# Expert layers of a two-layer decoder: the first pair's token rows are fetched from DRAM like those of the other seven pairs, instead of being packed by matrix products, and all row numbers are formed ahead of the pairs

## What is computed

```
lc   = xf @ w_coarse + b_coarse          # 4 groups; the best one is taken, with its softmax weight
lf   = (xf @ w_fine + b_fine)[that group]  # 4 experts of the group; the best two, softmax over the two
comb = sum of one_hot(expert) * weight   # [280 tokens, 16 experts], two entries a row
h    = silu(xf @ w_gate[e]) * (xf @ w_up[e])     # 1024 -> 256, for each expert e
y    = sum over e of (h * comb[:, e]) @ w_down[e]  # 256 -> 1024
```

## Time and profile before

| | |
|---|---|
| median of three runs | 1041.59 us |
| the profiled execution | 1038.86 us |
| its span, first to last instruction | 1037.2 us |
| mean granted clock of TensorE | 0.904 of 2.4 GHz |
| PE busy | 905.3 us (87%) |
| DVE busy | 462.8 us (45%) |
| ACT busy | 238.0 us (23%) |
| POOL busy | 180.1 us (17%) |
| moved by DMA | 165.33 MB, mean 159 GB/s |
| experts of layer 0, first gate product to last down product | 266.3 to 394.3 us |
| experts of layer 1, the same | 874.7 to 1003.5 us |

### The profile page before, as it was taken

How to read it: one execution, slowest core, us unless ns; L and a number is a source line. 1 busy time by engine, 2 the same in 40 slices (tenths; PEclk the granted TensorE clock), 3 DMA queues, 4 the chain that set the end, 5 groups by cost and what they waited for, 6 DMA issues and landing times.

```text
span 1037.2 us, 17012 instructions
## 1 busy us (share of the span) xinstructions
PE 905.3 (87%) x6716; PEld 669.5 (65%) x6716; DVE 462.8 (45%) x1015; ACT 238.0 (23%) x520; POOL 180.1 (17%) x215
## 2 busy tenths in 40 slices
PE   5895997797999998999889869889758988999995
PEld 3684875576665665777677668767534867565663
DVE  1697962525232434147854465533423134133424
ACT  0131222014011112254323312220632033111013
POOL 4104126000330001000069300001730001600000
PEclk9996988796899999999999889955879988899997
DMA  9452512062599994331000100001744442999901
GB/s 317 168 172 46 130 53 78 15 230 92 220 425 423 424 345 153 122 105 64 1 15 2 57 1 1 3 1 51 220 144 163 152 173 84 411 424 423 411 17 42
DMA packets 80237, 165.33 MB, mean 159 GB/s; under 512 B 20257, under 2 KB 58584, under 8 KB 71266
## 3 DMA queue, kind: packets, MB, share of 16 engines
q1 hardware_dynamic: 68348, 149.43, 39.0%
q0 software_dynamic: 6496, 14.24, 4.6%
q10 hardware_dynamic: 5312, 0.54, 0.4%
HBM read 156.02 MB, written 6.99 MB: 157 GB/s over the span
## 4 chain that ended last, share of the span: by engine, by line
PE 65%; DVE 19%; SPq 4%; issue 3%; ACT 3%; ACTq 2%; POOL 2%; DMA 1%; DVEq 0%
PE bank L1992 11%; DVE scratch L2089 7%; PE bank L2036 6%; PE bank L2024 6%; PE bank L1620 6%; PE bank L1890 5%; SPq L1563 3%; DVE scratch L2092 2%; ACTq L2483 2%; PE bank L793 2%; PE bank L1921 2%; PE bank L1839 2%; PE bank L811 2%; PE bank L1834 1%; PE bank L658 1%
## 5 line engine op out<-in xcount | busy, mean ns | idle before, releaser
L1620 PE MATMUL bank<-x_fm,weight_slots 128*128 128x280 f32 x576 | 144.1, 412 | 4.2 <-ACT x_fm L2563 2.8
L2487 ACT ACTIVATE scratch<-bank 128x280 f32<-128x280 f32 (+5 forms) x118 | 55.2, 478 | 344.7 <-PE bank L2024 111.9
L1620 PEld LDWEIGHTS bank<-x_fm,weight_slots 128*128 128x128 f32 x576 | 112.8, 197 | 33.1 <-issue 4.7
L1992 PE MATMUL bank<-weight_slots,scratch 128*64 128x256 f32 x672 | 92.6, 379 | 0.0
L2089 DVE TENSOR_TENSOR scratch<-bank,scratch 128x256 f32<-128x256 f32 x16 | 6.8, 425 | 156.3 <-PE bank L1992 156.3
L1992 PEld LDWEIGHTS bank<-weight_slots,scratch 128*64 128x64 f32 x672 | 58.4, 137 | 25.3 <-issue 4.6
L2089 DVE TENSOR_TENSOR scratch<-scratch 128x64 f32<-128x64 f32 (+13 forms) x94 | 55.5, 609 | 29.3 <-ACT scratch L2487 27.0
L2036 PE MATMUL bank<-scratch 128*128 128x280 f32 x256 | 66.3, 406 | 1.4 <-ACT scratch L2487 1.4
L1890 PE MATMUL bank<-scratch,weight_slots 128*128 128x280 f32 x256 | 63.1, 409 | 4.9 <-DVE scratch L2089 4.9
L1890 PEld LDWEIGHTS bank<-scratch,weight_slots 128*128 128x128 f32 x256 | 49.9, 196 | 17.6 <-DVE scratch L2089 5.3
L1533 POOL DMA_DIRECT2D scratch<-in_cache_krope x64 | 34.3, 537 | 154.5 <-ACT scratch L1427 136.6
(11 more groups left out here) (415 smaller groups left out, 1439.7 us busy)
## 6 DMA issues: line engine op xcount, KB each, us to landing
weight_slots<-in_moe_w_down SPq DMA_DIRECT2D x24, 1024.0 KB, 11.8
weight_slots<-in_moe_w_up SPq DMA_DIRECT2D x22, 1024.0 KB, 10.6
weight_slots<-in_moe_w_gate SPq DMA_DIRECT2D x20, 1024.0 KB, 11.2
scratch<-in_moe_w_gate SPq DMA_DIRECT2D x12, 1024.0 KB, 10.3
scratch<-in_moe_w_up SPq DMA_DIRECT2D x10, 1024.0 KB, 11.4
weight_slots<-in_od_w_in SPq DMA_DIRECT2D x9, 1024.0 KB, 5.5
weight_slots<-in_ev_w_in SPq DMA_DIRECT2D x8, 1024.0 KB, 12.5
scratch<-in_moe_w_down SPq DMA_DIRECT2D x8, 1024.0 KB, 13.0
```

Of the source, the lines that this page charges most:

```text
L1620: ins = pe.matmul(b[:, 0:NT], w[:, k, P * m2:P * m2 + P], src[:, k, :], start=(k == 0), stop=(k == kt - 1))
L1992: ins = pe.matmul(b[CAP * j:CAP * j + CAP, 0:DE], XG[:, q % 2, k, CAP * j:CAP * j + CAP], w[j][:, k, :], start=(k == 0), stop=(k == KD - 1))
L2487: return act.activation(dst, b[:rows, 0:width], f, **kw).then_inc(ring.free, 1)
```

## The change

Pair 0 goes the way of the other pairs. The products of `pack`, the tile `XTM3`, the copies of 24 rows of tokens and of `PICK` to other partitions on ACT, and the constant that went with them are removed; the third tile of tokens is stored like the other two. The row numbers of all eight pairs are formed in three steps (pair 0, pairs 1 to 3, pairs 4 to 7), each pair's as soon as its table is there, and all of them ahead of `turn(0)`. POOL waits for three marks instead of two and issues eight fetches instead of seven in each layer.

```diff
-        XTM, XTM3 = part(2240, 2, KD, P), part(4288, 2, P)
+        XTM = part(2240, 3, KD, P)
...
             def weighted(l): # POOL
-                pool.wait_ge(ev("rows_out"), 48 + 96 * (l + 1))
-                for q in range(1, NQ):
-                    if q in (1, 4):
+                pool.wait_ge(ev("rows_out"), 48 + 48 * (l + 1))
+                for q in range(NQ):
+                    if q in (0, 1, 4):
                         pool.wait_ge(*mark[f"rows{l}_{q}"])
                     if q == 4:
                         weights_of(l, 0)
-                    if q >= 5:
+                    if q >= 4:
                         pool.wait_ge(ev(f"rows_in{q % 4}"), rows_landed(l, q - 4))
                     pool.indirect_dma_start(YG[:, q, :], None, x_dram, ...)
...
 # PE
-                    pe.matmul(b[:, NE * t:NE * t + NE], cst("before32" if t == 2 else "before")[:r, :], one(t), start=(t == 0), stop=True)
+                    pe.matmul(b[:, NE * t:NE * t + NE], cst("before")[:r, :], one(t), start=(t == 0), stop=True)
...
-                def pack(q, half):
-                    ...
                 def rows_of_slots(q0, q1):
-                    pe.wait_ge(ev("dispatch_ready"), NG * l + (q1 - 1) // 2 + 1)
                     b = V.claim()
                     for q in range(q0, q1):
+                        pe.wait_ge(ev("dispatch_ready"), NG * l + q // 2 + 1)
...
-                pack(0, 0)
-                pack(0, 1)
+                rows_of_slots(0, 1)
                 rows_of_slots(1, 4)
+                rows_of_slots(4, NQ)
+                turn(0)
                 for q in range(NQ):
                     ...
-                    if q == 0:
-                        rows_of_slots(4, NQ)
...
 # DVE
-                dve.wait_ge(ev("pick_spread"), 3 * l + 3)
                 b = V.take()
                 s.do(dve.scalar_tensor_tensor(PLACE, b[:, 0:3 * NE]..., 1.0, PICK, ALU.add, ALU.mult))
...
                 dispatch(0)
+                row_numbers(0, 1)
+                dispatch(1)
+                row_numbers(1, 4)
+                dispatch(2)
+                dispatch(3)
+                row_numbers(4, NQ)
                 s.do(dve.tensor_reduce(CNT[:, 0:1], CNT, AX.X, ALU.max))
                 s.do(dve.tensor_scalar(OVER[:, l:l + 1], ...), ev("over_known"))
-                dispatch(1)
                 ...
-                dispatch(2)
-                dispatch(3)
                 packed(0)
-                row_numbers(1, 4)
...
 # ACT
-                        if t < 2:
-                            act.activation(XTM[:r, t, :, 64 * h:64 * h + 64], ...)
-                        else:
-                            for c in range(4):
-                                ins = act.activation(XTM3[32 * c:32 * c + r, :, 64 * h:64 * h + 64], ...)
-                            ins.then_inc(a_free, 1)
+                        act.activation(XTM[:r, t, :, 64 * h:64 * h + 64], b[:r, 0:512].rearrange("r (p k) -> r k p", k=KD), ACT.Copy).then_inc(a_free, 1)
...
-                act.wait_ge(ev("pick_ready"), l + 1)
-                for c in range(1, 4):
-                    act.activation(PICK[32 * c:32 * c + TT[2][1], 2, :], PICK[0:TT[2][1], 2, :], ACT.Copy).then_inc(ev("pick_spread"), 1)
...
 # SP
-                for t in range(2):
-                    sp.dma_start(x_dram[P * t:P * t + P, :], XTM[:, t]...)
-                for c in range(4):
-                    sp.dma_start(x_dram[2 * P:NT, :]...[c], XTM3[32 * c:32 * c + TT[2][1]])
+                for t, (c0, r) in enumerate(TT):
+                    sp.dma_start(x_dram[c0:c0 + r, :], XTM[:r, t].rearrange("p k f -> p (k f)")).then_inc(ev("rows_out"), 16)
```

More of the change, by code:

```diff
@@ L68 @@
           ("off2", P), ("off4", P), ("off8", P), ("off16", P),
-          ("scan", NPR), ("causal", P), ("curmask", 2 * NB), ("rank", 4), ("eps", 4), ("before", P), ("before32", P), ("iota", CAP), ("tokens", 3)]
+          ("scan", NPR), ("causal", P), ("curmask", 2 * NB), ("rank", 4), ("eps", 4), ("before", P), ("iota", CAP), ("tokens", 3)]
 COFF = {}
@@ L118, in const_table @@
     c["before"] = (a < b).astype(float)
-    c["before32"] = (a < b % 32).astype(float)
     c["iota"] = np.broadcast_to(np.arange(1, CAP + 1)[None, :].astype(float), (P, CAP))
@@ L425, in rows_landed @@
         def rows_landed(l, q):
-            return 16 * sum((m, k) <= (l, q) for m in range(2) for k in range(1, NQ) if k % 4 == q % 4)
+            return 16 * sum((m, k) <= (l, q) for m in range(2) for k in range(NQ) if k % 4 == q % 4)
         kt_read, score_banks = {}, {}
@@ L2389, in row_numbers @@
                     s.mark(dve.tensor_copy(ROWOF[:, q0:q1], b[:, q0:q1]), v_free)
+                    mark[f"rows{l}_{q0}"] = (v_free, V.n)
                 def packed(q):
-                    if q == 0:
-                        for c in range(4):
-                            empty(XG[:, q % 2].rearrange("p (half c) f -> p c half f", c=4)[:, c], 2 * P)
-                    else:
-                        for half in range(2):
-                            empty(XG[:, q % 2, 4 * half:4 * half + 4, :].rearrange("p c f -> p (c f)"), 512)
-                dispatch(0)
+                    for half in range(2):
+                        empty(XG[:, q % 2, 4 * half:4 * half + 4, :].rearrange("p c f -> p (c f)"), 512)
+                dispatch(0)
+                row_numbers(0, 1)
[4 more added lines that the diff above has]
+                row_numbers(4, NQ)
                 s.do(dve.tensor_reduce(CNT[:, 0:1], CNT, AX.X, ALU.max))
                 s.do(dve.tensor_scalar(OVER[:, l:l + 1], CNT[:, 0:1], CAP + 0.5, None, ALU.is_gt), ev("over_known"))
-                dispatch(1)
                 dve.wait_ge(ev("lc_exp"), 2 * l + 1)
@@ L2431, in out_and_moe @@
                     s.mark(mul(HB[:, q % 2, :], b[:, 0:DE], SIL[:, q % 2, :]), h_free)
-                    if q == 0:
-                        row_numbers(4, NQ)
-                        mark[f"rows{l}_4"] = (v_free, V.n)
                     if q < NQ - 1:
@@ L2664, in x_rows @@
                 sp.wait_ge(*mark[f"x_tok{l}"])
-                for t in range(2):
-                    sp.dma_start(x_dram[P * t:P * t + P, :], XTM[:, t].rearrange("p k f -> p (k f)")).then_inc(ev("rows_out"), 16)
-                for c in range(4):
-                    sp.dma_start(x_dram[2 * P:NT, :].rearrange("r (half c f) -> c r half f", half=2, c=4)[c], XTM3[32 * c:32 * c + TT[2][1]]).then_inc(ev("rows_out"), 16)
+                for t, (c0, r) in enumerate(TT):
+                    sp.dma_start(x_dram[c0:c0 + r, :], XTM[:r, t].rearrange("p k f -> p (k f)")).then_inc(ev("rows_out"), 16)
             def over_capacity_sp(l):
```

19 lines of the change are left out of this document (removed).

## The result

The changed kernel takes **1056.3 us** (median of four runs, 1053.7 to 1058.2) against 1042.3 for the kernel before in the same comparison (four runs, 1038.4 to 1046.3): ratio 1.0132, 95% interval 1.0087 to 1.0177. It is slower by 1.3%, 13.9 us, where +3.1 had been forecast, and lies outside the range. The profiled execution is 1056.61 us, its span 1054.9.

What follows compares the result with a forecast made beforehand. PE was taken as the bound, with 65% of the chain. Delayed gate products and clock loss, less removed row numbers and recovered down products, gave +1.7 and +1.4, together +3.1: 1044.7 us against the median, range 1034 to 1052.

Steps and rivals of the forecast that it cites:

- The terms of the experts: Gains and losses around pair 0 in each layer's expert stage: +1.7 us in layer 0, +1.4 in layer 1.
- fetch 0: POOL's fetch for pair 0 in layer 0: issued at 258.0, with 9.9 us to land at no cost.
- row numbers done: PE's row numbers of all pairs, ahead of pair 0's transposes: 0.22 us a record, done at 267.9 in layer 0.
- first gate product: Pair 0's first gate product starts later: 270.85 instead of 266.35 in layer 0 (+4.5 us), +5.5 in layer 1.
- the router's 20 columns: Router products left the clock at 0.50 without a pause, so one-column row numbers were expected to leave it there too.
- their loss: Pair 0's gate and up products start at a low clock and lose 2.1 us a layer, bounds 0 and 2.8.
- The down products gave back: Pair 0's down products, without one-column work ahead, get back 1.5 us in layer 0 and 2.8 in layer 1.
- The fetch: Pair 0's fetch lands 4 to 9 us after issue, within the 9.9 us available, so it costs nothing.
- The full clock: Rival, 15%: clock stays at or returns to 1.00 during the row numbers; together -8.5 us, 1033.
- The late fetch: Rival, 12%: pair 0's transposes wait for POOL's fetch; at a 17.2 us landing +17.7, 1059.
- Later pairs do not gain or lose: Expert pairs after pair 0: fetches issued sooner or at the same distance, refills follow the gate products; no change.
- Together +3.1: Sum over both layers' expert stages, +1.7 and +1.4: +3.1 us for the whole kernel.

Runs made afterwards that it cites:

- e4: Changed kernel with the row numbers of pairs 4 to 7 back behind the gate and up products of pair 0: 1061.9 us, ratio 1.0197 to the kernel before.
- e8: Changed kernel with 20 extra one-column products (80 instructions) in a PE wait long before the experts: 1047.5 us, ratio 1.0049 to the kernel before.
- e11: Changed kernel with 20 one-column products (80 instructions) in a PE wait of layer 1's mixer, 50 us ahead of the burst: 1050.5 us, ratio 1.0067.
- e3: Changed kernel leaving out 8 records of layer 0's down products (pairs 3 and 4), so the mixer is reached as early as before: 1052.2 us, ratio 1.0085.
- e10: Changed kernel with 10 extra one-column products (40 instructions) in a PE wait long before the experts: 1053.9 us, ratio 1.0141 to the kernel before.
- e9: Kernel before with 44 extra one-column products (176 instructions) in two PE waits of layer 0's mixer: 1049.9 us, ratio 1.0080.

## Why the prediction was wrong, point by point

**The terms of the experts: right.** Places at 253.98 (253.84 forecast); fetch 0 at 258.23 (258.0); row numbers done at 268.8 (267.9), since a record took 0.244 and not 0.22 (24 in 5.85), inside the bounds; first gate product at 271.80 (270.85). Relative to the router's start that is +5.5 and +5.9 instead of +4.5 and +5.5. The clock was at 0.50 through all row numbers and the transposes, as argued from the router's 20 columns, and came back 2.9 us into the gate products: their loss is 8.52 - 7.06 = 1.5 instead of 2.1. The down products gave back 1.4 and 2.7. Sum, measured over whole stages: +1.9 and +1.7 against +1.7 and +1.4.

**The fetch: right.** It lands in 4.2 us at the shortest and is covered by 10 us of row numbers. The Trainium skill's estimate for it ("DMA: Bandwidth & Descriptors", anatomy of a DMA on the GpSimd path) was 3.2; the trace has 1.0 more, and either is covered. e4 shows that this cover is needed.

**The rivals.** The full clock did not come (0.50 in three windows). The late fetch did not. What came was on nobody's list.

**The step that failed** is the sentence "Later pairs do not gain or lose" with the sum that ends there: "Together +3.1". It took the program outside the touched lines as a constant. That holds for the other pairs (down products of pair 2 at 3.58 in both kernels), not for the mixer of layer 1. Removing 68 instructions a layer moved the blocks in which PE's instructions come, and one now comes too late in a burst. As measured: +3.65 in the experts; +6.2 in the burst and the 50 records behind it, where PE stands still for 1.70 us and then runs at half the clock; and the remaining 4 of the 13.9 elsewhere, by the one profile in the part of the mixer ahead of the burst. The medians say the same less sharply: without the pause the changed kernel is at +5.1 (e8) to +7.0 (e11) instead of +13.9, and a made pause of 1.18 us in the kernel before brings 6.1 (interval 4.2 to 8.1).

The range ended at 1052, and with +3.65 alone the result would have been inside it. That the forecast of the touched stretch came out within 0.6 us is in part luck: the gate products come a microsecond later than forecast in layer 0, and lose less to the clock than the 2.1 put down for them.

**Open:** where those 4 us come from. The part ahead of the burst takes 252.4 to 257.6 us in the kernel before and its repeats, 259.4 and 259.5 in the changed kernel and its repeat, at a clock of 0.96 and 0.93; it was 256.1 in e3 and only 254.0 in e10. Moved fetches that stop PE less visibly, the later start, and chance from execution to execution all remain. e10's profile, with the pause and a mixer of only 451.9, is the fastest of its four runs, which go from 1049.7 to 1059.9.

## What to carry to other kernels

Taking instructions out of PE's stream, or putting some in, moves the fetches of everything behind; after any such edit look for "issue" rows in the middle of dense bursts of small products, far from the edit too, before the edit itself is blamed or praised. Here the burst had 192 records and a block 128 of them, so a block could both begin and end in it. A pause of one or two microseconds there is dear because the clock falls behind it: a few cheap products in an earlier wait can move the break away, and here that is worth 0.6 to 0.8%. One-column products are cheap in small groups and dear in long ones: behind 12 records in a row the down products ran at 1.00 (3.65 us), behind 24 they began at 0.50 (5.06 and 6.34).

## What the runs showed of the hardware that had not been expected

- PE's instructions come by the queue "q8 instruction" in packets of 16.4 KB, here 55 in the whole run, and 56 in e9, which has 176 instructions more. A break in a burst of 32x64 float32 products costs 1.63 to 2.01 us of standstill, and it moves by 20 records for 40 instructions (e10) and 8 for 16 (e3). With the break at record 130 or further there is a pause, at 117 or nearer, by count, there is none.
- 1.18 us without work in such a burst was followed by 9.8 us at 0.50 of the clock with PE fully busy, as were the 1.70 us of the changed kernel. Burst and 50 records behind it took 12.2 to 13.6 us in the seven runs with a pause and 7.3 in the nine without.
- A one-column float32 product with 128 x 128 weights takes 0.244 us a record at 0.50 (24 in 5.87) and 0.14 at 1.00 (24 in 3.37); at 0.50 a transpose of 128 columns takes the same (8 in 1.97).
